# Compact 64x64 blocks in the chunked recurrence of a two-model kernel, in place of 128x128 matrices with zero quadrants

## The reference, cut to what matters

```python
S = S * decay(t)                       # per channel of the key
S = S - (S k~) b~^T + v k^T            # remove along k~, write v k^T
y = S r
```

## Time and profile before

| | |
|---|---|
| Median of three runs | 2539.52 us (2538.29, 2539.52, 2552.52) |
| Profiled execution, first to last instruction | 2524.9 us |
| Median less span (what lies around the span) | 14.6 us |
| TensorE busy, share of the span | 2412.5 us, 96% |
| VectorE busy, share of the span | 1537.1 us, 61% |
| The two stretches of the recurrence's ladder | about 1257 to 1350 us and 1816 to 1910 us |

### The profile page before, as it was taken

One profiled execution on the slowest core, in us unless ns is written; L12 is line 12 of the kernel. 1 busy time (PEld: TensorE's weight loads), 2 busy tenths in 40 slices (PEclk: granted clock), 3 DMA queues, 4 the chain that ended last, 5 costly groups with the idle time before them and its releaser, 6 DMA issues.

```text
span 2524.9 us, 39563 instructions
## 1 busy us (share of the span) xinstructions
PE 2412.5 (96%) x14971; PEld 2013.5 (80%) x14971; DVE 1537.1 (61%) x3352; ACT 1080.7 (43%) x1971; POOL 0.2 (0%) x4
## 2 busy tenths in 40 slices
PE   7998999999899899999999899899999899999998
PEld 3853678888774899997798899897898788778885
DVE  4567453333477666657676666656766655558893
ACT  3236342223236655533403555542303554557882
POOL 0000000000000000000000000000000000000000
PEclk8999999999999999999999999999999999999999
DMA  9236423333226566543324466443322655459997
GB/s 338 88 127 239 148 84 100 93 100 96 80 89 223 175 200 192 168 150 105 97 76 138 139 193 198 147 129 97 101 72 84 223 186 175 142 197 354 329 358 271
DMA packets 182492, 410.08 MB, mean 162 GB/s; under 512 B 20256, under 2 KB 20512, under 8 KB 181792
## 3 DMA queue, kind: packets, MB, share of 16 engines
q1 hardware_dynamic: 182304, 407.56, 49.3%
HBM read 406.43 MB, written 1.05 MB: 161 GB/s over the span
## 4 chain that ended last, share of the span: by engine, by line
PE 89%; DVE 7%; ACT 1%; issue 1%; DMA 1%; SPq 0%; DVEq 0%; ACTq 0%
PE bank L822 11%; PE bank L826 11%; PE bank L825 11%; PE bank L1055 9%; PE bank L784 6%; PE bank L1072 5%; PE bank L1076 5%; PE bank L1075 5%; PE bank L842 3%; PE bank L846 2%; PE bank L845 2%; PE bank L911 2%; PE bank L982 2%; PE bank L1030 2%; PE bank L1207 1%
## 5 line engine op out<-in xcount | busy, mean ns | idle before, releaser
L2256 DVE TENSOR_TENSOR WL<-ring,WH 128x512 fp32r<-128x512 f32 x632 | 412.1, 687 | 250.9 <-ACT WH L1620 249.6
L1620 ACT ACTIVATE WH<-ring 128x512 fp32r<-128x512 f32 x632 | 375.4, 625 | 300.1 <-PE bank L822 207.1
L2341 DVE TENSOR_TENSOR WLE<-slots,WHE 128x1024 fp32r<-128x1024 f32 x231 | 281.2, 1223 | 123.1 <-ACT WHE L1620 119.9
L1620 ACT ACTIVATE WHE<-slots 128x1024 fp32r<-128x1024 f32 x231 | 244.6, 1061 | 114.6 <-PE bank L1072 113.9
L822 PE MATMUL bank<-AH,WH 128*128 128x256 f32 (+1 forms) x864 | 272.5, 315 | 1.3 <-DVE WL L2256 1.3
L826 PE MATMUL bank<-AH,WL 128*128 128x256 f32 (+1 forms) x864 | 271.9, 315 | 0.0
L825 PE MATMUL bank<-AL,WH 128*128 128x256 f32 (+1 forms) x864 | 270.7, 313 | 0.0
L1055 PE MATMUL bank<-X,ring 128*128 128x256 f32 x1024 | 245.9, 387 | 0.0
L1055 PEld LDWEIGHTS bank<-X,ring 128*128 128x128 f32 x1024 | 188.6, 191 | 34.1 <-issue 7.6
L826 PEld LDWEIGHTS bank<-AH,WL 128*128 128x128 f32 x864 | 162.2, 188 | 12.7
L822 PEld LDWEIGHTS bank<-AH,WH 128*128 128x128 f32 x864 | 162.3, 188 | 12.2 <-issue 1.5
(11 more groups left out here) (355 smaller groups left out, 4776.5 us busy)
## 6 DMA issues: line engine op xcount, KB each, us to landing
ring<-stream SPq DMA_DIRECT2D x992, 256.0 KB, 2.8
slots<-experts SPq DMA_DIRECT2D x264, 512.0 KB, 5.1
con<-consts SPq DMA_DIRECT2D x1, 3204.0 KB, 14.4
X<-xin SPq DMA_DIRECT2D x1, 2048.0 KB, 10.1
par<-params SPq DMA_DIRECT2D x1, 1302.5 KB, 7.1
LAST<-final_rows SPq DMA_DIRECT2D x1, 1024.0 KB, 5.5
out<-ZO SPq DMA_DIRECT2D x4, 256.0 KB, 2.0
con<-consts SPq DMA_DIRECT2D x1, 132.0 KB, 2.8
```

Source lines behind the costliest of these rows:

```text
L1620: return nc.scalar.activation(o, i, fn, **kw)
L2256: V.tensor_tensor(WL[:, s % SPLIT, :], ring[:, c % RING, :], WH[:, s % SPLIT, :].bitcast(F32), ALU.subtract).then_inc(w_taken, 1)
L2341: V.tensor_tensor(WLE[:, s % PAIR_SPLIT, :], pair(pair_of(s)), WHE[:, s % PAIR_SPLIT, :].bitcast(F32), ALU.subtract).then_inc(pair_taken, 1)
```

## The change

One head's two chunks of a pair no longer form a 128x128 matrix with two zero quadrants. Chunk c = 0 lies on partitions 0 to 63 and chunk c = 1 on partitions 64 to 127, each a 64x64 block of 64 columns, so `MM`, `XX`, `LK` and `PP` have half the columns. Each 128x128 matmul of a pair becomes two 64x64 ones, c = 0 in the upper left quadrant of the array and c = 1 in the lower right, written to the two partition halves of the same bank. The masks shrink alike. The last level computes only the transposed X, which alone is used after it. VectorE's operations have half the elements, or there are half as many; `GTN` is written in two operations in place of one.

```diff
-    ("pairmask", 512), ("inv0", 128), ("inv0t", 128), ("levels", 640), ("segs", 256), ("iota8", 8),
+    ("pairmask", 256), ("inv0", 64), ("inv0t", 64), ("levels", 320), ("ident64", 64), ("segs", 256), ("iota8", 8),
...
+        def rows_of(c):
+            return slice(c * HD, (c + 1) * HD)
+        def chunk_cols(n):
+            return slice(n * HD, (n + 1) * HD)
...
-                for m in (0, 4, 1, 5, 2, 6, 3, 7):
-                    b0, cp, j = m // 4 * HD, m // 2 % 2, m % 2
-                    tok = slice(cp * P, (cp + 1) * P)
-                    b = unit_begin()
-                    rhs = KR[b0:b0 + HD, j, :, tok]
-                    mm(b[:, 0:256].rearrange("p (a b) -> p a b", a=2), BH[b0:b0 + HD, j, tok], rhs, True, True)
-                    mm(b[:, 256:512].rearrange("p (a b) -> p a b", a=2), KH[b0:b0 + HD, j, tok], rhs, True, True, True)
+                for cp in range(2):
+
+                    bs = [unit_begin() for _ in range(2)]
+                    for j, n, c, par in product(range(2), range(2), range(2), range(2)):
+                        b0, tok = par * HD, chunk_cols(2 * cp + c)
+                        o = bs[par][rows_of(c), (2 * j + n) * P:(2 * j + n + 1) * P].rearrange("p (a b) -> p a b", a=2)
+                        mm(o, (BH, KH)[n][b0:b0 + HD, j, tok], KR[b0:b0 + HD, j, :, tok], True, True,
+                           j == 1 and n == 1 and c == 1)
                 bs = [unit_begin() for _ in range(2)]
-                for h, par in product(range(4), range(2)):
...
-                    mm(bs[par][:, h * P:(h + 1) * P], KR[b0:b0 + HD, j, 0, tok], BH[b0:b0 + HD, j, tok], True, True, h == 3)
+                for h, c, par in product(range(4), range(2), range(2)):
...
+                    mm(bs[par][rows_of(c), h * HD:(h + 1) * HD], KR[b0:b0 + HD, j, 0, tok], BH[b0:b0 + HD, j, tok],
+                       True, True, h == 3 and c == 1)
...
                 for lev in range(5):
                     ready_wait()
-                    for q in range(2):
-                        b = unit_begin()
-                        for h in range(4):
-                            m = 4 * q + h
-                            mm(b[:, h * P:(h + 1) * P], LK[:, m, :], XX[:, m, 0:P], True, True, h == 3)
+                    b = unit_begin()
+                    for m, c in product(range(8), range(2)):
+                        mm(b[rows_of(c), m * HD:(m + 1) * HD], LK[rows_of(c), m, :], XX[rows_of(c), m, 0:HD], True, True,
+                           m == 7 and c == 1)
                     gates(LEVEL_GATES)
                     branches(int(2 * lev < KD))
                     ready_wait()
-                    for q in range(4):
+                    if lev < 4:
+                        for q in range(2):
+                            b = unit_begin()
+                            for h, c in product(range(4), range(2)):
+                                m = 4 * q + h
+                                xt, pp = XX[rows_of(c), m, HD:2 * HD], PP[rows_of(c), m, :]
+                                mm(b[rows_of(c), 2 * h * HD:(2 * h + 1) * HD], xt, pp, True, True)
+                                mm(b[rows_of(c), (2 * h + 1) * HD:(2 * h + 2) * HD], pp, xt, True, True, h == 3 and c == 1)
+                    else:
+
                         b = unit_begin()
...
+                        for m, c in product(range(8), range(2)):
+                            mm(b[rows_of(c), m * HD:(m + 1) * HD], PP[rows_of(c), m, :], XX[rows_of(c), m, HD:2 * HD], True, True,
+                               m == 7 and c == 1)
...
-                    for q in range(2):
-                        free(V.tensor_copy(PP[:, 4 * q:4 * q + 4, :].rearrange("p a b -> p (a b)"), take()[:, :]))
+                    free(V.tensor_copy(PP[:, :, :].rearrange("p a b -> p (a b)"), take()[:, :]))
```

More of the change, by code:

```diff
@@ L1543, in _ @@
                 b = unit_begin()
[L1544 to L1551, removed]
+                for m, c in product(range(8), range(2)):
+                    mm(b[rows_of(c), m * HD:(m + 1) * HD], MM[rows_of(c), m, 2 * HD:3 * HD],
+                       TOK[3][rows_of(c), m // 2 % 2, head_cols(m)], True, True, m == 7 and c == 1)
+                bs = [unit_begin() for _ in range(2)]
+                for n, par, c in product(range(4), range(2), range(2)):
+                    b0, m = par * HD, 4 * par + n
+                    mm(bs[c][b0:b0 + HD, n * HD:(n + 1) * HD], TOK[0][rows_of(c), n // 2, head_cols(m)],
+                       XX[rows_of(c), m, HD:2 * HD], True, True, n == 3 and par == 1)
                 gates(SCAN_OPEN[0])
@@ L1554, in _ @@
                 b = unit_begin()
-                for m in range(8):
-                    mm(b[:, m * 64:(m + 1) * 64], XX[:, m, P:2 * P], MVS[:, m, :], True, True, m == 7)
+                for m, c in product(range(8), range(2)):
+                    mm(b[rows_of(c), m * HD:(m + 1) * HD], XX[rows_of(c), m, HD:2 * HD], MVS[rows_of(c), m, :], True, True,
+                       m == 7 and c == 1)
                 gates(SCAN_OPEN[1])
@@ L2791, in _ @@
                     free(V.tensor_copy(TOK[n][:, :, :].rearrange("p a b -> p (a b)"), take()[:, :]))
[L2792 to L2796, removed]
+                for m in (0, 4, 2, 6):
+                    free(V.tensor_tensor(MM[:, m:m + 2, :], take()[:, :].rearrange("p (a b) -> p a b", a=2),
+                                         over(cn("pairmask"), 2), ALU.mult))
+                for par in range(2):
+                    b = take()[:, 0:T].rearrange("p (m c) -> p m c", m=4)
+                    free(V.tensor_tensor(XX[:, 4 * par:4 * par + 4, 0:HD], b, over(cn("inv0"), 4), ALU.mult))
                 settled()
-                link(V.tensor_tensor(XX[:, :, P:2 * P], MM[:, :, 0:P], over(cn("inv0t"), 8), ALU.mult))
+                link(V.tensor_tensor(XX[:, :, HD:2 * HD], MM[:, :, 0:HD], over(cn("inv0t"), 8), ALU.mult))
                 xx = XX[:, :, :].rearrange("p m (a c) -> p (m a) c", a=2)
-                link(V.tensor_tensor(xx, xx, over(ident, 16), ALU.add))
+                link(V.tensor_tensor(xx, xx, over(cn("ident64"), 16), ALU.add))
                 for lev in range(5):
-                    link(V.tensor_tensor(LK, MM[:, :, 0:P], over(cn("levels", lev * P, (lev + 1) * P), 8), ALU.mult))
+                    link(V.tensor_tensor(LK, MM[:, :, 0:HD], over(cn("levels", lev * HD, (lev + 1) * HD), 8), ALU.mult))
                     go()
@@ L2812, in _ @@
                     branches(l, int(2 * lev < KD))
-                    for q in range(4):
-                        x2 = XX[:, 2 * q:2 * q + 2, :].rearrange("p a b -> p (a b)")
-                        free(V.tensor_tensor(x2, x2, take()[:, :], ALU.subtract))
+                    if lev < 4:
+                        for q in range(2):
+                            x2 = XX[:, 4 * q:4 * q + 4, :].rearrange("p a b -> p (a b)")
+                            free(V.tensor_tensor(x2, x2, take()[:, :], ALU.subtract))
+                    else:
+                        xt = XX[:, :, HD:2 * HD]
+                        free(V.tensor_tensor(xt, xt, take()[:, :].rearrange("p (a b) -> p a b", a=8), ALU.subtract))
                     settled()
@@ L2818, in _ @@
                 free(V.tensor_copy(MVS[:, :, :].rearrange("p a b -> p (a b)"), take()[:, :]))
-                free(V.tensor_scalar(GTN[:, :, :].rearrange("p a b -> p (a b)"), take()[:, :], -1.0, None, ALU.mult))
+                for c in range(2):
+                    free(V.tensor_scalar(GTN[:, :, chunk_cols(c)], take()[:, 0:T].rearrange("p (a b) -> p a b", a=4), -1.0, None, ALU.mult))
                 settled()
@@ L2912, in _unit_bases @@
         u += 8 + len(PAIRS) - KD
-        u += 6 + 2 + 4 + 8 + 2 + 5 * 6 + 3 + 20 + 2
+        u += 6 + 2 + 4 + 4 + 2 + 4 * 3 + 2 + 4 + 20 + 2
         out[l]["merge"] = u
```

31 lines of the change are left out of this document (14 added, 17 removed).

## The result

The changed kernel takes 2510.48 us in the median of four executions (2501.61 to 2512.43), the kernel before 2538.9 (four executions): a ratio of 0.9876, 95% interval 0.9843 to 0.9909, 28.4 us less. Later, on another chip, six executions of the change against eleven of before gave 2503.81 and 2533.42 us, ratio 0.9887 (0.9858 to 0.9916). The forecast was 2511.0 us.

A forecast was written before the change was run, and what follows sets the result against it. TensorE was taken to bound both ladders; block savings summed to 14.27 us a layer, 28.5 for both, so the span of 2524.9 becomes 2496.4 and, with 14.6 around it, 2511.0 us. Range 2507 to 2520.

The forecast's parts named there:

- The bound: In both ladders TensorE is the limit, busy 92.84 of 93.00 us; VectorE's saving by itself is worth nothing.
- The prediction's own term for this stretch: From the transposes to the levels, where VectorE frees the banks: 1.9 to 2.9 us saved a layer, 2.4 taken.
- The price of a block: Any 64x64 block costs 0.35 + 0.0575 n us, n being the records on its busiest quadrant.
- a term of 10.4: Five levels, saved a layer: first halves 2.55 us, second halves of levels 1 to 4 5.52, last second half 2.30.
- The two open terms: MVS and GTN, 0.99 us saved a layer (0.76 to 1.22); transposes to levels, 2.4 (1.9 to 2.9).
- The covers: VectorE's go stays in time: slack 0.9 us in second halves; first level's go at 1271.0, needed 1271.5 or later.
- No wait on `smalls`: Sign in the profile after: TensorE would not wait on `smalls`, as weight streaming has room for a 15% shorter ladder.
- Strict order of the code: Rival: quadrants overlap only in code order, second halves take 3.11 us, kernel 2519.9 us; chance 0.13.
- Turns on one bank: Rival: in the levels, rows writing the same bank exclude each other, 2540.4 us, no change; chance 0.04.
- A block without overlap: Rival: longer new blocks, above all second halves, get no quadrant overlap, 2552.5 us, slower than before; chance 0.03.
- a wait on VectorE in a second half: Rival: VectorE's answer 0.5 us later than held in each second half, 4 us lost, about 2515 us; chance 0.05.

The follow-up runs named there:

- experiment 4: Changed kernel, LK masking repeated in levels 2 to 5: twice, every block and filler unchanged to 0.01 us; four times, 8.7 us more in both layers.
- experiment 5: Changed kernel with level blocks on all four quadrants: 2493.95 us, ratio 0.9838; with MVS and U0N spread too: 2486.09 us, ratio 0.9816.
- experiment 1: Changed kernel, same matmuls reordered per quadrant: eight in a row, first half 1.83 us, second 3.34; four in a row, 1.47 and 2.61.
- the runs of four: Changed kernel with level blocks ordered as four matmuls to one quadrant, then four to the other: first half 1.47 us, second half 2.61.
- the four-quadrant version: Changed kernel with matrices 4 to 7 written to the other partition half of a second bank, VectorE moving them back: 2493.95 us, ratio 0.9838.

## Why the prediction was right, point by point

**The bound.** From the first level on it is TensorE's blocks and nothing else: 11.9 of the 14.7 us a layer are TensorE's time there, and experiment 4 shows from both sides that VectorE's saving is worth nothing in the levels. Ahead of them it is not so, and the prediction's sentences that TensorE waits for 0.16 us only and that VectorE's saving is by itself worth nothing do not hold there. In the old block of 32 records the first eight start within 0.87 us, then a unit of four is completed every 0.60 us, which is the pace of VectorE's takes (4.86/8), though the row shows TensorE as busy. At the pace of its first eight records the block would have taken some 3.8 us, an estimate, and it took 5.46. The prediction's own term for this stretch counted with that pace. Had VectorE still taken eight banks there, faster matmuls alone would have gained little of its 2.76 us; no run separates the two parts.

**The price of a block,** 0.35 + 0.0575 n, was worked out from two blocks of the scan and carried to n = 32. A first half costs 1.08 and 0.19 of stretched filler, 1.27, as predicted. A second half costs 2.06 and 0.19, 2.25 for 2.19; 0.04 of the 0.07 too much in the block is a late start of one quadrant's sixth record (0.099 us behind its fifth, where 0.058 is the rule), for which I know no cause. Over the five levels 50.97 us (1274.43 to 1325.40) became 40.86 (1273.26 to 1314.12): 10.1 saved for a term of 10.4.

**The two open terms** both lie at or near their four-quadrant side. MVS, GTN and U0N with their fillers went from 8.29 us (1325.40 to 1333.69) to 6.47 (1314.12 to 1320.59), 1.82 for 1.50 (MVS and GTN 1.21, the upper end of their range, U0N 0.61 for 0.51). From the first transpose to the first level 16.69 us became 13.93, 2.76 for 2.4. I took the middle since no row had four quadrants at once; four at once is right (1.54 us for n = 24, and experiment 5). These two terms were too small by 0.7 us a layer and the levels too large by 0.3, so the sum of 14.3 a layer was 0.4 short. What I did not see is the start of the first pair of chunks, 0.22 us later behind the transposes than before, 0.15 of it since both banks are waited for at once.

**The covers.** Go ahead of need by 1.2 us in the trace, 0.9 predicted, as the 0.19 us of stretched filler, priced as a cost, also give VectorE time; the first level's go came at 1269.92 for a block at 1273.26. No wait on `smalls`, as predicted.

**The rivals.** Strict order of the code would have cost 2.91 us a second half (0.15 + 48 x 0.0575); the block took 2.06. But the rival was nearer than the argument against it told: experiment 1 shows a look-ahead of about three records, the change uses all three of them, and the earlier trace rows showed only that a single record is passed. By the Trainium skill ("TensorE: Matmul & The Clock Gate", Part 3: Packing small matmuls) matmuls start strictly in program order; the 1.47 us of the runs of four, where strict order of starts gives 1.82, disagree. Turns on one bank would give first halves of 2 us; they take 1.08, so for row halves that write different partition halves of one bank the rule of "TensorEngine Tiling (Array Packing)" in the Trainium skill, Restrictions and Gotchas, does not hold in this trace. Row halves that write the same partitions of one bank were not tried; the four-quadrant version gives them a bank each. A block without overlap, and a wait on VectorE in a second half, did not occur.

**The step that was wrong** and did no harm: I took 14.6 us as time around the span, as the table of the kernel before does. The profiled execution of the change took 2501.61 us with a span of 2499.8, so 1.8 us lie around it. The rest was the draw: the profile of before shows an execution that was some 13 us faster than the median. Since I took a difference off both, this dropped out; a forecast made from the absolute span (2496.4 + 1.8) would have been off by twelve. That the median then came out right to 0.5 us is luck beyond what the working can claim: the interval of the measurement reaches from 23 to 40 us saved, and the ladders say 29.4.

## What to carry to other kernels

Price a block of small matmuls by the records on its busiest quadrant, plus a fixed cost for every change of the array's shape, and take both from two blocks of different length in the trace; then spread the matmuls over all four quadrants, as VectorE can bring a half back from the other partitions of PSUM where it has slack. Look at who frees the banks as well: a row can show TensorE as busy while VectorE sets its pace. Change quadrant after at most two fp32 matmuls (four records), since the look-ahead is short. And where executions scatter by more than the change, match the traces by instruction and read the stretch that the change touches; it repeated here to a hundredth of a microsecond.

## What the runs showed of the hardware that I had not expected

- The look-ahead past a busy quadrant is three matmul records: 2.8 from 1.83 us, it then gave 1.47 and 2.61 us for another order, and the starts of single records show the first record of the other quadrant 0.005 us after the thirteenth of sixteen, and 0.006 us after the fifth of eight.
- Four quadrants together take 64 records in 1.09 us, one in 0.015 us without the fixed part (0.94/64), at the same 0.0575 us a record on each quadrant.
- A full stationary operand costs 0.11 us a record whether 64 or 128 columns follow (1.73 and 1.78 us for 16), a 64x64 one 0.0575.
- Entering and leaving the 64x64 shape costs 0.34 us, even for a single matmul.
- The same code took up to 21 us more or less ahead of the first ladder from one execution to another (1256.5 to 1277.8 us), at a mean granted clock of 0.97 in both. One stretch of it without waits took 280.00 us in place of 274.67 at a granted clock of 1.00; the cause is open.
- In a stage with waits behind the second ladder the granted clock was 0.81 in one execution and 1.00 in the other, and the same 20 records were busy 1.69 us longer.
